# Two groups of sample heads computed inside the latent heads' preparation, and a head norm beside another group's prompt attention

## The reference

```
h = rmsnorm(x)
[FoX | SWA | MLA inputs] = h @ w_in
FoX: 6 heads of 64, scores + (cumulated gates of the query - those of the key)
SWA: 6 query heads on 2 key heads, window of 128 frames, a sink per head, a bias by distance
MLA: 4 heads; q = rmsnorm(cq) @ w_uq, k and v = rmsnorm(ckv) @ w_ukv, rotated parts,
     then a norm of every head of q and k with gains g_mla_q, g_mla_k
x += w_out( [rms(FoX) | rms(SWA) | rms(MLA)] * g_mix_out )
x += ConvFFN(rmsnorm(x))
```

## Time and profile before

| | |
|---|---|
| median of three runs | 3229.61 us (3228.44 to 3230.09) |
| the profiled execution | 3231.43 us |
| its span | 3229.7 us |
| mean granted clock of TensorE over the span | 0.938 |
| busy: PE, DVE, ACT, POOL | 2960.0, 1578.2, 999.4, 919.6 us |

### The profile page before, as it was taken

The page is one execution under the profiler, slowest core; times in us unless marked ns, Lnnn a source line. Parts: engine busy times, 40 slices in busy tenths (PEclk is TensorE's granted clock), DMA queues, the critical chain, the costliest instruction groups (busy, mean ns, idle before and its releaser), DMA issues. The chain is left out here.

```text
span 3229.7 us, 51941 instructions
## 1 busy us (share of the span) xinstructions
PE 2960.0 (92%) x20656; PEld 2770.8 (86%) x20656; DVE 1578.2 (49%) x2747; ACT 999.4 (31%) x2259; POOL 919.6 (28%) x538
## 2 busy tenths in 40 slices
PE   6998877689999999999999998776899999999998
PEld 6997755379999999999999975645699999999998
DVE  3336555763344444444452574657443444444443
ACT  4334435553311111111243263455343111111111
POOL 3112134133422322322231123332243322223220
PEclk9998968798999999999999998787899999999999
DMA  5120100003411111111211201000133111111111
GB/s 162 39 68 23 40 11 18 1 14 100 153 40 52 46 45 39 52 39 42 69 65 38 77 2 41 11 18 1 34 120 126 52 39 39 52 39 52 39 52 55
DMA packets 181253, 161.86 MB, mean 50 GB/s; under 512 B 17236, under 2 KB 168316, under 8 KB 180860
## 3 DMA queue, kind: packets, MB, share of 16 engines
q1 hardware_dynamic: 181116, 160.02, 15.8%
HBM read 129.97 MB, written 30.13 MB: 50 GB/s over the span
## 5 line engine op out<-in xcount | busy, mean ns | idle before, releaser
L2059 PE MATMUL bank_b<-x_hi,fwhi 128*128 128x352 f32 x2112 | 689.3, 326 | 5.3 <-POOL fwlo L2015 5.3
L2059 PE MATMUL bank_b<-x_hi,fwlo 128*128 128x352 f32 x2112 | 687.5, 326 | 0.0
L2059 PE MATMUL bank_b<-f_lo,fwhi 128*128 128x352 f32 x2112 | 685.9, 325 | 0.0
L2015 POOL TENSOR_TENSOR fwlo<-raw,fwhi 128x1024 fp32r<-128x1024 f32 x132 | 321.8, 2438 | 578.7 <-ACT fwhi L2140 568.2
L2059 PEld LDWEIGHTS bank_b<-x_hi,fwhi 128*128 128x128 f32 x2112 | 398.8, 189 | 6.6 <-POOL fwlo L2015 5.9
L2059 PEld LDWEIGHTS bank_b<-f_lo,fwhi 128*128 128x128 f32 x2112 | 401.1, 190 | 0.0
L2059 PEld LDWEIGHTS bank_b<-x_hi,fwlo 128*128 128x128 f32 x2112 | 397.8, 188 | 0.6
L2248 DVE TENSOR_TENSOR fx<-fx,bank_b 128x352 f32<-128x352 f32 x528 | 275.8, 522 | 242.6 <-PE bank_b L2089 242.6
L2089 PE MATMUL bank_b<-fuhi,fwhi 128*128 128x352 f32 x1056 | 343.8, 326 | 4.5 <-DVE fulo L2242 4.5
L2089 PE MATMUL bank_b<-fulo,fwhi 128*128 128x352 f32 x1056 | 345.3, 327 | 0.0
L2089 PE MATMUL bank_b<-fuhi,fwlo 128*128 128x352 f32 x1056 | 344.7, 326 | 0.0
(11 more groups left out here) (428 smaller groups left out, 6025.6 us busy)
## 6 DMA issues: line engine op xcount, KB each, us to landing
raw<-in_w_ffn_up SPq DMA_DIRECT2D x88, 512.0 KB, 3.8
raw<-in_w_ffn_down SPq DMA_DIRECT2D x44, 512.0 KB, 3.5
wraw<-in_w_in SPq DMA_DIRECT2D x18, 984.0 KB, 5.4
xs<-x_between SPq DMA_DIRECT2D x16, 528.0 KB, 3.9
x_between<-xs SPq DMA_DIRECT2D x16, 528.0 KB, 2.7
fx<-x_between SPq DMA_DIRECT2D x2, 4224.0 KB, 12.5
raw<-in_w_out SPq DMA_DIRECT2D x16, 512.0 KB, 5.3
x_between<-fx SPq DMA_DIRECT2D x3, 1408.0 KB, 5.7
```

Of the source, the lines that this page charges most:

```text
L2015: pool.tensor_tensor(self.wlo[:, r], self.raw[:, o % 2], self.whi[:, r].bitcast(F32), ALU.subtract)\
L2059: last = pe.matmul(bank[:, first_bank + t, 0:TN], w[:, role, c, :], x[:, c, self.cols(t)], start=(c == 0 and m == 0), stop=(c == DC - 1 an ...
```

## The change

The stages 2 and 4 are gone. Their work is now in a class `SampleHeads`, and a new function `latents_and_samples`, which takes the place of `mla_prepare`, calls it from the 17 steps m of the preparation: PE transposes two tiles of FoX's keys in each of the steps 0 to 5 and SWA's in 6, scores in 7 and 8 (first four heads) and 10 and 11 (the other two), transposes probabilities in 12 to 15, and mixes the values behind the last step. ACT and DVE take the transposed tiles in turn. To make room the PSUM tiles of the preparation are single: one bank each of psX, psQ, psK and psO, three for the scores, one for the transposes. Small tensors lie in columns of `proj` that are no longer needed.

The caches (FoX's keys and values, the latents) are loaded during SWA's prompt attention. SWA's head norm moves from stage 2 into FoX's prompt attention, in 9 squares, 9 sums and 27 products by tile. The squares of `MixedNorm` are cut into eight parts, two of them the 32 sample columns. The scale of the cache's keys (L1613) moves from the end of the preparation into MLA's prompt attention, on POOL still. The query gain (L1709) is dropped there and folded into the copies of MLA's prompt and sample attention, where a scalar_tensor_tensor takes the place of a tensor_tensor. MLA's sample attention gets a function of its own with the same steps. The semaphores of the first layer's entry get a restart block of their own, to make room for others.

```diff
+def latents_and_samples(nc, k, lay, places, proj, qm, km, vm, mixed, yT, fs, caches):
+        psX, psQ, psK, psO = bank("mpsX"), bank("mpsQ"), bank("mpsK"), bank("mpsO")
...
+            @block.tensor
+                smp.turn_queries(pe)
+                turn(0)
+                for m in range(KT):
+                    project(m)
+                    if m + 1 < KT:
+                        turn(m + 1)
+                    if m < 6:
+                        smp.turn_fox_keys(pe, 2 * m)
+                        smp.turn_fox_keys(pe, 2 * m + 1)
+                    elif m == 6:
+                        smp.turn_swa_keys(pe)
+                    elif m in (7, 10):
+                        smp.score_fox(pe, m // 10)
+                    elif m in (8, 11):
+                        smp.score_swa(pe, m // 11)
+                    elif 12 <= m < 16:
+                        smp.turn_probs(pe, smp.PROBS + 2 * (m - 12))
+                        smp.turn_probs(pe, smp.PROBS + 2 * (m - 12) + 1)
+                smp.all_taken(pe)
+                smp.mix_swa(pe)
+                smp.mix_fox(pe)
+                mixed.sums(pe, (psX, psK))
...
+            @block.scalar
+                for m in range(KT):
+                    if m + 1 < KT:
+                        copy_turned(m + 1)
+                    act.activation(km[0:n, j, :, 0:NOPE], kv[:, :, 0:NOPE], ACT.Copy)
+                    act.activation(vm[0:n, j, :, :], kv[:, :, NOPE:], ACT.Copy).then_inc(k_out, 1)
+                    act.activation(sqk[m % NS][:, :, :], km[:, j], ACT.Square).then_inc(k_squared, 1)
+                    if m < 6:
+                        smp.take_fox_keys(act, copy, 2 * m)
...
 class MixedNorm:
     def pool_upto(self, pool, upto):
+        if self.keys:
+            v, inverse = self.keys
+            pool.tensor_tensor(v, v, inverse, ALU.mult).then_inc(self.keys_done, 1)
...
 class SwaHeads:
+    def pool_upto(self, pool, upto):
+        if upto >= 8 and not self.squared:
+            for t in range(TT):
+                own.after(pool.tensor_tensor(self.sq[:, t % 2], self.heads[:, t], self.heads[:, t], ALU.mult))
+        if upto >= 20 and not self.scaled:
+            pool.wait_ge(self.inverse_steps, 2)
+            for t in range(TT):
+                own.after(pool.tensor_tensor(v, v, bcast(self.ss[:, t], [P, self.NH, HD], 2), ALU.mult))
+                own.after(pool.tensor_tensor(v[:, 0:SWAH], v[:, 0:SWAH], row(R_SQ, SWAH), ALU.mult))
+                own.after(pool.tensor_tensor(v[:, SWAH:], v[:, SWAH:], row(R_SK, SWAKV), ALU.mult))
...
 def attend_prompt(...):
-                    dve.tensor_tensor(qT[1][0:kdim, r % RQ, :, :], psX[0:kdim, 0],
-                                      qT[0][0:kdim, r % RQ, :, :].bitcast(F32), ALU.subtract)
+                    hi = qT[0][0:kdim, r % RQ, :, :].bitcast(F32)
+                    if mla:
+                        dve.scalar_tensor_tensor(qT[1][0:kdim, r % RQ, :, :], psX[0:kdim, 0], gain, hi, ALU.mult,
+                                                 ALU.subtract)
```

## The result

The changed kernel takes 3205.27 us (median of four runs, 3203.33 to 3208.47): a ratio of 0.9917 to the kernel before, 95% interval 0.9905 to 0.9930 (the medians alone, 3205.27 and 3229.85, give 0.9924). Forecast were 3200 and a range from 3169 to 3232. The sign and the size were right, and the gain came where the forecast had it, from two chains side by side. Inside the sum two terms were off in opposite directions; that they nearly cancelled was luck.

The account below looks back on a forecast made before the run. PE bounds the whole span, but the rewritten stages are chains of waiting engines. A layer gains 154.4 - 12.5 - 120 - 6 = 15.9, two 31.8, less 1.8: 30.0 us, so 3200; range 3169 to 3232.

Parts of the forecast that it names:

- Two chains side by side cost less than both in a row: FoX's sample attention and the preparation, chains of waiting engines, merged: 154.4 us a layer becomes 120 plus 12.5 of boundaries.
- The merged stage, 120: Sample heads and preparation as one stage: nine summed parts along the chain that ends last, 119.8, taken as 120 us.
- first rival: The clock stays full in the merged stage, which takes 110 us; total 3180; chance .20.
- the six steps: Steps 0 to 5 of the merged stage: 6.5 us each, between 5.4 and 8.3 by clock, together 39.0.
- price of a step at full clock: One of steps 0 to 5: product, turn, ACT's copies and second key transposes in series, 5.4 us.
- signs of being wrong: Merged stage above 135 us, steps shorter than 5.4, or prompt attentions longer by more than 16 us together.
- DVE's list of 38 instructions: Behind the second scores: rotation, query sums, normalisations and probability copies run as one list at .48 each, 18.2 us.
- The prompt attentions, 3 each: FoX's takes in the head norm (0 to 10 us), MLA's POOL's key scale (0 to 5.5); 3 us taken for each.
- the rule that the prediction weighed: A DVE instruction with two SBUF inputs or in two-port mode and a GpSimd instruction reading SBUF exclude each other; excess 5.1.
- third rival: POOL locks DVE out in the prompt attentions: FoX's 10 us longer, MLA's 5.5; total 3218.6; chance .15.
- The restart for the first layer's entry, 1.8: The added semaphore restart block at the first layer's entry costs 1.8 us once.
- Boundaries, 1.8 and 8.9: FoX's prompt to SWA's and SWA's to the merged stage 1.8 us each; last scale to first matmul 8.9.

Follow-up runs that it names:

- second profile: The changed kernel run once more with nothing altered, ratio taken to the kernel before: 0.9923 (0.9904 to 0.9942), 3207.11 us.

## Why the prediction was right, and where it was not

- *Two chains side by side cost less than both in a row*: right. From FoX's prompt end to MLA's first matmul, without SWA's prompt attention, 154.5 us became 121.3 in the first layer and 151.7 became 126.9 in the second; forecast were 132.5. Taking the second layer as equal was wrong by 8.5 us of gain: its stretch before was 2.8 shorter, and its merged stage 5.6 longer, at a mean granted clock of .75 where the first's had .83 (last two windows of the first table of windows). In the changed kernel's second profile it was the other way round, so this is the clock of an execution and no property of the layer.
- *The merged stage, 120*: mis-sized. It took 107.9 (476.92 to 584.83) in the first layer, 113.5 in the second, and 114.8 and 110.7 in the second profile: 112 on average, close to the first rival's 110. In the first layer the six steps took 32.2 for 39.0, the scores 4.7 and 4.4 for 6.4 each, since the clock was 1.00 there and I had put it between the levels; the prediction's own price of a step at full clock, 5.4, held, and one of its signs of being wrong, steps under 5.4, came true by .15. That is the first rival's mechanism, in part: the mixing stayed at 0.50. The other terms came close: 4.4 for 5.7 at the start, 19.2 for the 19.8 from the second scores to the mixing, 16.3 for 15.5 of mixing, 7.5 for 8.2 of sums, 5.4 for 5.3 of scale, and what is left 13.8 for 13.5.
- *Its explanation as DVE's list of 38 instructions*: the 18.2 was right by size and at most in part by cause. Half of the list's time taken away shortened it by 2.5 and 3.2. What sets it beside DVE was not isolated.
- *The prompt attentions, 3 each*: mis-sized, by the rule that the prediction weighed. MLA's cost 5.2 and 6.3; moving the key scale away took 5.9 and 7.6 off, PE's wait for DVE and a lower clock together, which is the third rival's mechanism at about its price of 5.5. FoX's cost 5.6 and 5.8, against the rival's 10: by PE's idle time 3.2 are the nine sums, put into DVE's idle time at no price, 0.9 the products on POOL, and 1.2 stay open.
- *The restart for the first layer's entry, 1.8*: about 2.75. From DVE's last scale of the entry to its next instruction 8.7 us passed, before 5.9. The rest of the 3.75 lies mostly ahead of it, where executions of the changed kernel differ by more.
- *Boundaries, 1.8 and 8.9*: 2.0 and 9.5.

So the faster steps paid for the dearer prompt attentions: over two layers the merged stage gave 18.6 us more than the sum had, the prompt attentions took 10.9 more, and the remaining items, each small, took the rest. The sum landed 5 us off by these cancelling, which is luck. The first rival's clock and the third rival's lock both came true in part. The range had room for either.

## What to carry to other kernels

When work moves beside a stage that another engine bounds, ask whether long DVE and POOL instructions will read SBUF at the same time: a single POOL instruction of 5.5 us cost 6 to 8 a layer where DVE scaled in SBUF (3 of it a wait of PE), and nothing 20 us earlier, where DVE's inputs were in PSUM and POOL was idle. In a chain with single buffers, order each engine's copies by who waits for them; ACT's copy for PE, three places earlier, was worth about 1 us a step. Idle time of an engine, taken as a sum over a stage, is not room: DVE had 26 us of it and 5.7 us of sums still cost more than 3. Where the clock changes between executions, compare PE's idle time in a stage and not only its length.

## What was not expected of the hardware

FoX's mixing, matmuls with 64 moving columns, stayed at a granted clock of 0.50 with PE busy for all of 16.6 us. The same matmuls behind six sums of 352 and 320 columns ran at 1.00 in one layer and at a mean of 0.80 in the other. In the stage's first steps the clock was at 1.00 with PE busy for 21.5 of 32.0 us. So here the stretch with the larger busy share had the lower clock.
